# Moving eight transposition bursts on TensorE and one tanh on ScalarE in a two-layer hybrid SSD / gMLP step

## The chip, the cores and the metric

The kernel runs on one core of a Trainium2 chip. The metric is the device time of one execution in microseconds (us), the median of several runs. Engine names: TensorE (PE) does matmuls and transpositions and loads its weights beside them (PEld), VectorE (DVE) and ScalarE (ACT) work element by element, GpSimd (POOL) here only splits weights, SyncE (SP) and ScalarE issue transfers.

## The reference, cut to what matters

Two layers act on 640 tokens (128 context, 512 latent) of 1024 features. Each layer normalises, makes one wide input projection, and feeds two branches:

```python
h = rms_norm(x, norm_w) * (1 + scale[:, None]) + shift[:, None]
proj = h @ w_in
xbc_raw, z_m, dt_raw, u_raw, v_raw, z_g, gl_m, gl_g = split(proj)
# SSD branch: xs, bm, cm of 1024 + 512 + 512 channels
xbc = silu(dwconv(xbc_raw, conv_w, conv_b))          # 5 taps, centred
dt = softplus(dt_raw + dt_bias)
y = scan forward + scan backward + d_skip * xs       # chunks of 128 tokens
y_m = rms_norm(y * silu(z_m), ssm_norm_w)
# gMLP branch
v = layer_norm(gelu(v_raw), ln_w, ln_b)
y_g = gelu(u_raw) * (w_sp mixing of v over 128 tokens + b_sp) * silu(z_g)
merged = sigmoid(gl_m) * (y_m @ w_out_m) + sigmoid(gl_g) * (y_g @ w_out_g)
x = x + gate[:, None] * (merged @ w_out)
```

## The kernel before, in words

Every layer has 89 weight tiles p = 0 to 88, each 128 output channels of 1024 inputs. A float32 product is made of three products of rounded parts (`hi*hi`, `lo*hi`, `hi*lo`), so an ordinary tile (`tile`, L538, with `chunk`, L554) has 8 chunks of 3 x 2 = 6 matmuls of 320 columns: 48 matmuls. It accumulates in one of two PSUM buffers, `acc0` and `acc1`. Tile t takes them in turn by `acc_no(t)` (L53), and `acc_ready` (L501) makes TensorE wait on `acc_free` until the tile two turns back has been read out.

Tiles 0 to 24 are the first phase of a layer. Tile 1 is dt. `V_AT` (L43) lists the eight v tiles 4, 5, 10, 11, 16, 17, 23, 24: they are computed in pairs with tokens on the partitions (`v_tile`, L504), and a pair shares one `acc` buffer and half of a bank X1 or X3; ScalarE reads a pair out with one gelu of 1024 columns (L1117, which frees the buffer) and one of 256 (L1120, which raises `v_made`). The remaining sixteen, `CONV_AT` (L44), are conv tiles. For conv i ScalarE copies the tile to `raw` (L1139), VectorE makes five taps (L1549, L1551), ScalarE a tanh (`conv_tanh`, L1084 to L1089), and VectorE the product (L1567). In layer 1 the first three conv tiles are computed before the row scale is known and go another way to `raw` (`raw_conv`, L1034); `RAWT, NRAW = 4, 3` (L48) name them: tiles 0, 2 and 3. So in layer 1 the tanh of conv 2 belongs to tile 3.

The last eight convs, i = 8 to 15, give x0 to x7. VectorE writes each to one of two buffers, `xo[:, j % 2]`; a write for i >= 10 waits until x of two convs before has been transposed (`tp_ready`, L1565) and stored to memory (`xf_stored`, L1566). TensorE transposes x_j in five 128x128 pieces to banks X0 and X1 (`x_transposes`, L850; `transposes`, L715, L720), ScalarE copies them to `x_tok` (L964, L965) and issues two stores to `xf_dram` (L1081, L1082).

Where such side work stands within TensorE's tiles is a table: `X_AT` (L88) for the x transpositions, `A_AT` for the bursts that make the chunk states (`a_burst`, L749). An entry (p, k) means: inside tile p, after its chunk k; k = 8 is behind the tile's last chunk. The same table sets the order on ScalarE: at the end of its step for tile p it does `copies(p + 1)`, the copies of all bursts of tile p + 1. All engines run strictly in the order in which their code is written. GpSimd splits weights two tiles ahead, SyncE loads them.

ScalarE's functions live in tables, of which one set is loaded at a time: the program carries explicit ACT_TABLE_LOAD instructions where the next function is not in the set at hand.

Of the kernel before, what the change touches and what calls it, by code (L numbers as in the profile page):

```python
# [38 lines left out]
N_TILES = 1 + NCONV + 8 + 16 + 8 + 32 + 8  # L39
# [4 lines left out]
CONV_AT = tuple(p for p in range(25) if p != DT_AT and p not in V_AT)  # L44
# [3 lines left out]
RAWT, NRAW = 4, 3  # L48
# [10 lines left out]
def weight_at(p):  # L59
# [11 lines left out]
    if p >= T_ZM:  # L71
# [13 lines left out]
NU = len(A_UNITS)  # L85

A_AT = [(19 + a, 2) for a in range(7)] + [(26 + a // 3, 2 + 3 * (a % 3)) for a in range(14)]
X_AT = [(p + 2, 4) for p in CONV_AT[8:14]] + [(25, 3), (25, 6)]  # L88
V_BANK = (1, 1, 3, 1)
PBB_AT = (27, 8)  # L90
SP_AT = [(30, 4), (31, 4), (32, 4), (34, 4), (36, 4), (38, 4), (39, 6), (40, 6)]
# [1 line left out]
B_AT = [(T_G - 2, 4), (T_G - 1, 8)] + [(p, k + 1) for p, k in B_AT[2:]]  # L93
STANDS = sorted([(at, "a", n) for n, at in enumerate(A_AT)] + [(at, "x", n) for n, at in enumerate(X_AT)]
                + [(PBB_AT, "pbb", 0)]
# [63 lines left out]
def build(nc, xT, wts, wada, cT, bada, normw, finalw, ssmw, convw, dtb, alog, dskip, lnw, lnb,  # L159
# [126 lines left out]
    def sem(name):  # L286
        return ctx.enter_context(nc.semaphore(name))
# [23 lines left out]
    tp_ready, tp_out, ln_ready = sem("tp_ready"), sem("tp_out"), sem("ln_ready")  # L311
# [30 lines left out]
    def acc_of(t):  # L342
        return acc[acc_no(t) % 2]
# [16 lines left out]
    def evacuated(eng, t):  # L360

        eng.wait_ge(acc_free[acc_no(t) % 2], acc_no(t) // 2 + 1)
# [135 lines left out]
    def _(pe):  # L498
        mm = nc.tensor.matmul

        def acc_ready(t):  # L501
            pe.wait_ge(acc_free[acc_no(t) % 2], acc_no(t) // 2)

        def v_tile(t, half, ready=None, hooks=()):  # L504


            j = V_AT.index(t % N_TILES) // 2
            if half == 0:
                acc_ready(t)
                if j > 0:  # L510
                    pe.wait_ge(v_made, KC // 2 * (t // N_TILES) + j)
                if j == 3:
                    pe.wait_ge(tp_out, 8 * (t // N_TILES) + 6)
                if ready is not None:
                    pe.wait_ge(hpre_ready, 8 * (ready[2] + 1))
            a, s = acc_of(t), t % 2
            for i in range(KC // 2):
                k = KC // 2 * half + i
                if i % 2 == 0:
                    pe.wait_ge(w_split, WQ * t + 3 + i // 2)  # L520
                if ready is not None:
                    for r in ready[0:2]:
                        pe.wait_ge(r, 8 * ready[2] + k + 1)
                for c in range(NCH):
                    out = X[V_BANK[j]][:, 2 * P:4 * P] if c == NCH - 1 else \
                        a[:, c // 2, 2 * P * (c % 2):2 * P * (c % 2 + 1)]
                    for n, (w, x) in enumerate(((w_hi, h_hi), (w_lo, h_hi), (w_hi, h_lo))):
                        last = mm(out.rearrange("p (t n) -> p t n", t=2), x[:, k, P * c:P * (c + 1)],  # L528
                                  w[:, s, :].rearrange("p (t k n) -> p k t n", t=2, n=P)[:, i, :, :],
                                  start=(k == 0 and n == 0 and c % 2 == 0),  # L530
                                  stop=(k == KC - 1 and n == 2 and (c % 2 == 1 or c == NCH - 1)))
                    if i == KC // 2 - 1 and c == NCH - 1:
                        last.then_inc(tile_done, 1)
                    for at, hook in hooks:
                        if (at == 2 * i + 1 and c == 2) or (at == 2 * i + 2 and c == NCH - 1):
                            hook()
# [309 lines left out]
        for L in range(DEPTH):  # L846
# [3 lines left out]
            def x_transposes(j):  # L850
                pe.wait_ge(conv_done, NCONV * L + 9 + j)
                if X_AT[j][0] > V_AT[-1]:
                    pe.wait_ge(v_made, KC // 2 * (L + 1))
# [16 lines left out]
            for p in range(1 if L > 0 else DT_AT + 1, T_G):  # L870
# [7 lines left out]
                elif p in V_AT:  # L878
                    v_tile(T0 + p, V_AT.index(p) % 2, hooks=hooks,
                           ready=(hhi_ready, h_ready, L) if L > 0 and p < RAWT + 2 else None)  # L880
# [4 lines left out]
            for j in range(8):  # L885
                p = T_G + 2 * j
# [24 lines left out]
    def _(act):  # L911
# [3 lines left out]
        def free(t, ins):  # L915
            ins.then_inc(acc_free[acc_no(t) % 2], 1)
# [70 lines left out]
        for L in range(DEPTH):  # L987
# [13 lines left out]
            def dt_log():  # L1001
                act.wait_ge(dtu_ready, L + 1)
                A(dtx[:, 2, :, :], dtx[:, 1, :, :], ACT.Ln).then_inc(dtl_ready, 1)
# [80 lines left out]
            def conv_tanh(i):  # L1084
                n = NCONV * L + i
                act.wait_ge(cv_ready, n + 1)
                if n > 0:
                    act.wait_ge(conv_done, n)
                A(cvt[:, 0:CW], cv[:, i % 2, 0:CW], ACT.Tanh).then_inc(cvt_ready, 1)  # L1089
# [8 lines left out]
            for p in range(T_UZ):  # L1098
                t = T0 + p
                if L == 0 or p >= RAWT:  # L1100
                    act.wait_ge(tile_done, t + 1)
                if p == DT_AT:
                    if L == 0:
                        for dst, src in pieces(acc_of(t), *dt_row, L, 64):
                            last = A(dst, src, ACT.Identity, bias=dtb_sb[0:64, L:L + 1])
                        free(t, last)
                        evacuated(act, t)
                        act.sem_inc(dtrow_ready, 1)
                        conv_tanh(0)
                        dt_exp()  # L1110
                        dt_log()
                    continue
                if p in V_AT:
                    j, half = divmod(V_AT.index(p), 2)
                    if half == 1:
                        g = slice(2 * j, 2 * j + 2)
                        free(t, A(v_tok[:, g, 0:NCH - 1, :].rearrange("p g c n -> p c g n"),  # L1117
                                  acc_of(t)[:, :, :].rearrange("p b (c g n) -> p (b c) g n", c=2, n=P),
                                  ACT.Gelu_apprx_tanh))
                        A(v_tok[:, g, NCH - 1, :], X[V_BANK[j]][:, 2 * P:4 * P].rearrange("p (g n) -> p g n", n=P),  # L1120
                          ACT.Gelu_apprx_tanh).then_inc(v_made, 1)
                    if L > 0 and p == RAWT + 1:
                        conv_tanh(NRAW - 1)
                    copies(p + 1)
                    continue
                i = CONV_AT.index(p)
                if L > 0 and i < NRAW:
                    if i > 0:
                        raw_conv(i, p)
                        conv_tanh(i - 1)  # L1130
                        (dt_exp, dt_log)[i - 1]()
                        copies(p + 1)
                    continue
                if i >= 2:
                    act.wait_ge(cv_ready, NCONV * L + i - 1)
                else:
                    act.wait_ge(pads_ready, L + 1)
                for dst, src in pieces(acc_of(t), *raw_row(i), L):
                    last = A(dst, src, ACT.Copy)  # L1139
                free(t, last)  # L1140
                if i == (4, 5)[L]:
                    act.wait_ge(cum_ready, L + 1)
                    for d in range(2):
                        act.dma_start(cum_dram[L, NH * d:NH * (d + 1), :], cum_t[32 * d:32 * d + NH, :])\
                            .then_inc(cum_stored, 16)
                    act.wait_ge(ex_arg, L + 1)
                    A(ex[:, :, :, :], ex[:, :, :, :], ACT.Exp).then_inc(ex_ready, 1)
                    for rows in (slice(0, NH), slice(64, 64 + NH)):
                        A(c_buf[4][rows, :], cum_t[rows, :], ACT.Exp).then_inc(exr_ready, 1)
                    act.wait_ge(exr_ready, 2 * (L + 1))  # L1150
                    for d in range(2):
                        act.dma_start(ex_dram[L, :, d, :, :], c_buf[4][64 * d:64 * d + NH, :]).then_inc(ex_stored, 16)
                if i == 9:
                    act.dma_start(lnb_sb[:, :], lnb[L:L + 1, :].rearrange("l (k p) -> p (l k)", p=P),
                                  allow_slow_non_contiguous=True).then_inc(wsp_in, 16)
                    act.dma_start(states[0][:, :], h0[L, 0, :, :]).then_inc(st_in, 16)
                    act.dma_start(states[2 * (NCH - 2) + 1][:, :], h0[L, 1, :, :]).then_inc(st_in, 16)
                if L == 0 and i == 0:
                    continue
                copies(p + 1)  # L1160
                conv_tanh(i)
# [22 lines left out]
            for what, n in order_act():  # L1184
# [8 lines left out]
                elif what == "uz":  # L1193
                    t = T0 + T_UZ + n
# [13 lines left out]
                elif what == "glg":  # L1208
                    t = T0 + T_G + 2 * n
# [3 lines left out]
                else:  # L1213
# [6 lines left out]
                    if n < NU:  # L1220
# [4 lines left out]
                        for h in range(HPG):  # L1225
                            j = HPG * g + h
# [8 lines left out]
                        for h in range(HPG):  # L1235
                            j = NH + HPG * g + h
# [7 lines left out]
            for j in range(8):  # L1244
                t = T0 + T_ZM + j
# [13 lines left out]
            for j in range(8):  # L1259
                t = T0 + GLM_AT[j]  # L1260
# [676 lines left out]
```

## Time and profile before

| what | value |
|---|---|
| time, median of 3 (lowest to highest) | 1458.27 us (1458.12 to 1458.31) |
| time of the profiled execution | 1458.31 us |
| its span | 1456.2 us |
| TensorE busy | 1438.0 us, 99% |
| VectorE / ScalarE / GpSimd busy | 986.3 / 469.4 / 1029.5 us |
| TensorE clock over the run | 0.997 of full |

The profiled execution's own time is its span plus 2.1 us that lie around it. A row of the time line gives the start in us, the time in us that the row covers, the engine, the source line and operation, what it writes and reads, and the count; in brackets behind it stands how long the engine was idle before and who ended that.

### The profile page before, as it was taken

The page shows a single profiled execution, that of the slowest core. Times are in us where ns is not written, and L with a number is a line of the kernel's source. Part 1 is how long each engine was busy: PE and PEld are TensorE (multiplying, and loading weights), DVE is VectorE, ACT ScalarE, POOL GpSimd, SP SyncE. Part 2 cuts the span into 40 slices and gives each one's busy share as a digit, 9 for nine tenths or more (in the row PEclk, how much of TensorE's full clock was granted, in tenths as well). Part 3 has the DMA queues.
Part 4 walks back from the last instruction along what each step waited for, and adds up shares of the span by engine and source line. Part 5 has one row for each costly group of instructions (what it writes and reads, how often), then busy time and mean ns, then how long its engine had stood idle before and what let it go on. Part 6 is the DMA issues. An engine that isn't in the chain of part 4 may idle for free.

```text
span 1456.2 us, 26929 instructions
## 1 busy us (share of the span) xinstructions
PE 1438.0 (99%) x10127; PEld 1392.1 (96%) x10127; DVE 986.3 (68%) x1451; ACT 469.4 (32%) x1079; POOL 1029.5 (71%) x1431
## 2 busy tenths in 40 slices
PE   8999999999999999999999999999999999999996
PEld 5999998999999999999999999989999999999996
DVE  5865566674787678988869676567567885867234
ACT  4331222313666423001243323241256661310111
POOL 2688875596555489998868897658864556979762
PEclk9999999999999999999999999999999999999998
DMA  9112433113566465444342232411347655443222
GB/s 365 60 63 73 129 108 120 61 63 115 162 180 184 136 266 198 140 154 135 112 144 74 77 118 96 136 58 59 102 130 193 168 171 184 164 179 116 73 74 86
DMA packets 110988, 190.30 MB, mean 131 GB/s; under 512 B 10656, under 2 KB 72224, under 8 KB 109472
## 3 DMA queue, kind: packets, MB, share of 16 engines
q1 hardware_dynamic: 40448, 139.65, 28.8%
q10 hardware_dynamic: 70432, 49.11, 11.4%
q8 instruction: 80, 1.31, 0.4%
q14 instruction: 28, 0.23, 0.0%
HBM read 170.58 MB, written 18.15 MB: 130 GB/s over the span
## 4 chain that ended last, share of the span: by engine, by line
PE 95%; DVE 2%; issue 1%; POOL 0%; DMA 0%; ACT 0%; DVEq 0%; SPq 0%; POOLq 0%; ACTq 0%
PE acc L563 76%; PE acc L528 6%; PE X L795 2%; PE X L762 2%; PE X L787 2%; PE X L528 1%; PE X L827 1%; PE X L806 1%; PE X L720 1%; PE acc L573 1%; DVE cv L1551 1%; PE acc L679 0%; PE X L610 0%; DMA xr<-in_xT 0%; DVE xr L1852 0%
## 5 line engine op out<-in xcount | busy, mean ns | idle before, releaser
L466 POOL CAST w_hi<-w_st 128x256 fp32r<-128x256 f32 x708 | 413.7, 599 | 399.1 <-issue 180.7
L471 POOL TENSOR_TENSOR w_lo<-w_st,w_hi 128x256 fp32r<-128x256 f32 x708 | 653.3, 933 | 0.0
L563 PE MATMUL acc<-h_hi,w_hi 128*128 128x320 f32 x1744 | 406.3, 314 | 1.0 <-POOL w_lo L471 0.8
L563 PE MATMUL acc<-h_lo,w_hi 128*128 128x320 f32 x1744 | 397.8, 309 | 0.4 <-DVE h_lo L1408 0.4
L563 PE MATMUL acc<-h_hi,w_lo 128*128 128x320 f32 x1744 | 397.5, 309 | 0.0
L563 PEld LDWEIGHTS acc<-h_hi,w_hi 128*128 128x128 f32 x1744 | 288.6, 188 | 11.1 <-issue 7.6
L563 PEld LDWEIGHTS acc<-h_lo,w_hi 128*128 128x128 f32 x1744 | 291.5, 188 | 1.1 <-DVE h_lo L1408 0.9
L563 PEld LDWEIGHTS acc<-h_hi,w_lo 128*128 128x128 f32 x1744 | 291.4, 188 | 0.0
L1551 DVE SCALAR_TENSOR_TENSOR cv<-raw,convw_sb,cv 128x642 f32<-128x642 f32 x128 | 134.8, 1053 | 4.5
L1336 DVE SCALAR_TENSOR_TENSOR ada_acc<-ada_st,sc,ada_acc 128x512 f32<-128x512 f32 x112 | 103.4, 962 | 1.8
L1089 ACT ACTIVATE cvt<-cv 128x642 f32<-128x642 f32 x32 | 23.8, 743 | 159.4 <-DVE cv L1551 159.4
L528 PE MATMUL acc<-w_hi,h_hi 128*128 128x256 f32 x256 | 73.4, 287 | 0.3 <-POOL w_lo L471 0.3
L528 PE MATMUL acc<-w_hi,h_lo 128*128 128x256 f32 x256 | 72.4, 283 | 0.0
L528 PE MATMUL acc<-w_lo,h_hi 128*128 128x256 f32 x256 | 72.4, 283 | 0.0
L1632 DVE SCALAR_TENSOR_TENSOR gdt<-gm,tm,gdt 128x128 f32<-128x128 f32 x160 | 71.6, 507 | 1.1 <-ACT gdt L1237 0.8
L1532 DVE TENSOR_TENSOR xw<-x_tok,ex 128x256 f32<-128x256 f32 x80 | 46.0, 618 | 37.6 <-PE X L762 37.2
L1549 DVE TENSOR_SCALAR cv<-raw,convw_sb 128x642 f32<-128x642 f32 x32 | 27.3, 852 | 62.7 <-ACT raw L1139 62.6
L1227 ACT ACTIVATE dmat<-cum_bc,ncf 128x128 f32<-128x128 f32 x160 | 62.4, 390 | 15.3 <-issue 10.9
L1268 ACT ACTIVATE c_buf<-acc 128x640 f32<-128x640 f32 x16 | 11.3, 706 | 159.8 <-PE acc L563 159.8
L1229 ACT ACTIVATE cum_bc<-cum_bc,ebs 128x128 f32<-128x128 f32 x160 | 62.0, 387 | 0.0
L1237 ACT ACTIVATE gdt<-gm,tm 128x128 f32<-128x128 f32 x160 | 51.2, 391 | 27.8 <-DVE gm L1645 21.1
L563 PE MATMUL acc<-yg_hi,w_hi 128*128 128x320 f32 x256 | 60.1, 316 | 0.0
(256 smaller groups left out, 2493.9 us busy)
## 6 DMA issues: line engine op xcount, KB each, us to landing
w_st<-in_wts SPq DMA_DIRECT2D x178, 512.0 KB, 3.6
cum_bc<-cum_dram ACTq DMA_DIRECT2D x80, 256.0 KB, 5.0
ada_st<-in_wada SPq DMA_DIRECT2D x33, 512.0 KB, 4.3
ex_bc<-ex_dram ACTq DMA_DIRECT2D x64, 128.0 KB, 3.4
ada_pre<-in_wada SPq DMA_DIRECT2D x15, 512.0 KB, 13.2
mga_dram<-c_buf SPq DMA_DIRECT2D x16, 320.0 KB, 4.8
xf<-xf_dram SPq DMA_DIRECT2D x4, 1280.0 KB, 7.0
mga<-mga_dram SPq DMA_DIRECT2D x2, 2560.0 KB, 10.2
```

The costliest lines, as they stand in the source:

```text
L466: nc.gpsimd.tensor_copy(w_hi[:, slot, cols], w_st[:, slot, cols]).then_inc(s_pool, 1)
L471: nc.gpsimd.tensor_tensor(w_lo[:, slot, cols], w_st[:, slot, cols], f(w_hi[:, slot, cols]), ALU.subtract).then_inc(w_split, 1)
L528: last = mm(out.rearrange("p (t n) -> p t n", t=2), x[:, k, P * c:P * (c + 1)], w[:, s, :].rearrange("p (t k n) -> p k t n", t=2, n=P)[:, ...
L563: last = mm(a[:, hf, 0:n1], w[:, s, cols], x[:, k, hf * HALF:hf * HALF + n1], start=(k == 0 and n == 0), stop=(k == KC - 1 and n == 2))
L762: mm(X[3][:, cols], bt[:, s, :], xw[:, s, :, :, :].rearrange("p d h w -> p (d h w)")[:, cols], start=True, stop=True).then_inc(s_mm, 1)
L1227: last = A(dmat[:, n % 2, h, :], cum_bc[n % 2][:, 0, h, :], ACT.Identity, bias=ncf[:, c, j:j + 1])
L1229: last = A(cum_bc[n % 2][:, 1, h, :], cum_bc[n % 2][:, 1, h, :], ACT.Identity, bias=ebs[:, c, j:j + 1])
L1237: last = A(gdt[:, n % 2, h, :], gm[:, n % 2, 1, :], ACT.Copy, scale=tm[:, c, j:j + 1])
L1336: STT(out=o, in0=w, scalar=s, in1=o, op0=ALU.mult, op1=ALU.add)
L1532: last = TT(xw[:, a % 2, d, :, :], xg, per_head(ex[:, d, c, HPG * g:HPG * (g + 1)], HD), ALU.mult)
L1551: ins = STT(out=o, in0=r[:, tap:tap + CW], scalar=w[:, tap:tap + 1], in1=o, op0=ALU.mult, op1=ALU.add)
L1632: last = STT(out=gdt[:, s, h, :], in0=gm[:, s, 0, :], scalar=tm[:, c, j:j + 1], in1=gdt[:, s, h, :], op0=ALU.mult, op1=ALU.add)
```

## The change: what it does

Three edits.

1. `X_AT`: x0 to x4 move from behind chunk 4 to behind the last chunk of the same tile (15, 16, 17, 20, 21). x5 moves from tile 22, chunk 4, to tile 25, chunk 3; x6 from (25, 3) to (25, 5); x7 from (25, 6) to (25, 8).
2. `v_tile`: the wait on `tp_out` ahead of tile 23 goes. The `elif` changes nothing: `ready` is only given for the first pair.
3. ScalarE, layer 1: the tanh of conv 2 moves from behind the gelus of the pair 4, 5 to the step of tile 4, ahead of them.

```diff
-X_AT = [(p + 2, 4) for p in CONV_AT[8:14]] + [(25, 3), (25, 6)]
+X_AT = [(p + 2, 8) for p in CONV_AT[8:13]] + [(25, 3), (25, 5), (25, 8)]
...
                 if j > 0:
                     pe.wait_ge(v_made, KC // 2 * (t // N_TILES) + j)
-                if j == 3:
-                    pe.wait_ge(tp_out, 8 * (t // N_TILES) + 6)
-                if ready is not None:
+                elif ready is not None:
                     pe.wait_ge(hpre_ready, 8 * (ready[2] + 1))
...
                     j, half = divmod(V_AT.index(p), 2)
+                    if L > 0 and p == RAWT:
+                        conv_tanh(NRAW - 1)
                     if half == 1:
                         g = slice(2 * j, 2 * j + 2)
                         free(t, A(v_tok[:, g, 0:NCH - 1, :].rearrange("p g c n -> p c g n"),
...
                           ACT.Gelu_apprx_tanh).then_inc(v_made, 1)
-                    if L > 0 and p == RAWT + 1:
-                        conv_tanh(NRAW - 1)
                     copies(p + 1)
```

First place: ScalarE in layer 1, from the copy of tile 3 on, before the change. `cvt<-cv` is a conv's tanh, `dtx` the logarithm for dt, `v_tok` a gelu, `raw` the copy of a conv tile.

```order
L1037 ACTIVATE raw_71<-c_buf2_89,bsh_143 128x5x64
L1089 ACTIVATE cvt_73<-cv_72 128x642 [waits conv_done,cv_ready]
L1003 ACT_TABLE_LOAD
L1003 ACTIVATE dtx_94<-dtx_94 128x160 [waits dtu_ready]
L1117 ACT_TABLE_LOAD [waits tile_done]
L1117 ACTIVATE v_tok_55<-acc1 128x4x2x128 [waits tile_done]
L1120 ACTIVATE v_tok_55<-X1 128x2x128
L1089 ACTIVATE cvt_73<-cv_72 128x642 [waits conv_done,cv_ready]
L1139 ACTIVATE raw_71<-acc0 128x128 [waits cv_ready,tile_done]
```

The same stretch of ScalarE with the change (lines move by two).

```order
L1035 ACTIVATE raw_71<-c_buf2_89,bsh_143 128x5x64
L1087 ACTIVATE cvt_73<-cv_72 128x642 [waits conv_done,cv_ready]
L1001 ACT_TABLE_LOAD
L1001 ACTIVATE dtx_94<-dtx_94 128x160 [waits dtu_ready]
L1087 ACT_TABLE_LOAD [waits conv_done,cv_ready]
L1087 ACTIVATE cvt_73<-cv_72 128x642 [waits tile_done]
L1117 ACT_TABLE_LOAD
L1117 ACTIVATE v_tok_55<-acc1 128x4x2x128 [waits tile_done]
L1120 ACTIVATE v_tok_55<-X1 128x2x128
L1137 ACTIVATE raw_71<-acc0 128x128 [waits cv_ready,tile_done]
```

The tanh of conv 2 now stands ahead of the gelu that reads `acc1`, a third table load has come in, and the load ahead of the tanh carries the waits of the tanh.

Second place: TensorE, the border of tiles 6 and 7 in layer 1; these rows are the same before and with the change (here before).

```order
L563 MATMUL acc0<-h_hi_49,w_lo_54 128x320 x2
L563 MATMUL acc0<-h_lo_50,w_hi_53 128x320 x2
L563 MATMUL acc1<-h_hi_49,w_hi_53 128x320 [waits w_split,acc_free1]
L563 MATMUL acc1<-h_hi_49,w_hi_53 128x320
L563 MATMUL acc1<-h_hi_49,w_lo_54 128x320 x2
```

Tile 7 writes `acc1`, which the pair 4, 5 has used, and its first matmul waits for the release of that buffer.

Third place: TensorE in tile 25 (buffer `acc1` in layer 0) with the change, from the burst behind its third chunk on. L718 is a transposition burst.

```order
L718 MATMUL X1<-ident_118,xo_74 128x128 [waits tp_out,v_made,conv_done]
L718 MATMUL X0<-ident_118,xo_74 128x128 x4
L561 MATMUL acc1<-h_hi_49,w_hi_53 128x320 x2
L561 MATMUL acc1<-h_hi_49,w_lo_54 128x320 x2
L561 MATMUL acc1<-h_lo_50,w_hi_53 128x320 x2
L561 MATMUL acc1<-h_hi_49,w_hi_53 128x320 [waits w_split]
L561 MATMUL acc1<-h_hi_49,w_hi_53 128x320
L561 MATMUL acc1<-h_hi_49,w_lo_54 128x320 x2
L561 MATMUL acc1<-h_lo_50,w_hi_53 128x320 x2
L718 MATMUL X1<-ident_118,xo_74 128x128 [waits tp_out,v_made,conv_done]
L718 MATMUL X0<-ident_118,xo_74 128x128 x4
```

Before, the first of these bursts was x6, and x7 followed three chunks behind it; now they are x5 and x6, two chunks apart, and x7 closes the tile.

## Rows read from the trace of the kernel before

**Rows 1.** The page: busy time (us, share of span), and the chain's shares.

```profile
PE 1438.0 (99%) x10127; PEld 1392.1 (96%) x10127; DVE 986.3 (68%) x1451; ACT 469.4 (32%) x1079; POOL 1029.5 (71%) x1431
PE 95%; DVE 2%; issue 1%; POOL 0%; DMA 0%; ACT 0%; DVEq 0%; SPq 0%; POOLq 0%; ACTq 0%
```

**Rows 2.** Waits of TensorE, whole span: waiter, releaser, us, times, longest.

```profile
PE acc L617 <- DVE sel L1382: 3.2, 1, 3.2
...
PE X L762 <- ACT bt L1074: 0.5, 2, 0.2
```

**Rows 3.** Time line of TensorE, layer 1, around the starts of tiles 6 and 7.

```profile
783.26 0.28 PE L528 MATMUL X<-w_hi,h_lo 128*128 128x256 f32 x1
783.38 0.46 PE L563 MATMUL acc<-h_hi,w_hi 128*128 128x320 f32 x2
...
790.42 0.46 PE L563 MATMUL acc<-h_hi,w_hi 128*128 128x320 f32 x2
```

**Rows 4.** Time line of ScalarE, 783 to 799 us.

```profile
784.16 1.28 ACT L1003 ACT_TABLE_LOAD   x1
785.46 0.34 ACT L1003 ACTIVATE dtx<-dtx 128x160 f32<-128x160 f32 x1
785.81 1.28 ACT L1117 ACT_TABLE_LOAD   x1
787.11 1.03 ACT L1117 ACTIVATE v_tok<-acc 128x1024 f32<-128x1024 f32 x1
...
794.19 0.74 ACT L1089 ACTIVATE cvt<-cv 128x642 f32<-128x642 f32 x1 [5.78 <-DVE cv L1551]
794.83 1.32 ACT L1139 ACTIVATE raw<-acc 128x128 f32<-128x128 f32 x3
```

**Rows 5.** Time line of VectorE, 783 to 796 us.

```profile
785.83 1.15 DVE L1487 RECIPROCAL dtx<-dtx 128x160 f32<-128x160 f32 x1 [0.39 <-ACT dtx L1003]
...
789.46 0.61 DVE L1549 TENSOR_SCALAR cv<-raw,convw_sb 128x642 f32<-128x642 f32 x1
790.10 4.05 DVE L1551 SCALAR_TENSOR_TENSOR cv<-raw,convw_sb,cv 128x642 f32<-128x642 f32 x4
```

**Rows 6.** Busy us by engine; the PEclk column after POOL is the granted clock.

```profile
0.00:5.00 5.00, 1.77 (x4) 1.51 (x5) 1.08 (x6) 1.50 (x2) 2.00 (x13) 1.00 0.55 163
...
1446.00:1447.00 1.00, 0.54 (x3) 0.30 (x3) 0.80 (x3) 0.17 (x1) 0.00 (x0) 1.00 0.00 0
1447.00:1448.00 1.00, 0.00 (x0) 0.00 (x0) 1.00 (x3) 0.00 (x0) 0.00 (x0) 0.53 0.00 0
```

**Rows 7.** Time line of TensorE, layer 0, tile 25: burst x6; start of tile 26.

```profile
226.54 0.71 PE L720 MATMUL X<-ident,xo 128*128 128x128 f32 x5
...
232.03 0.46 PE L563 MATMUL acc<-h_hi,w_hi 128*128 128x320 f32 x2
```

**Rows 8.** Time line of ScalarE, layer 0, 223 to 231 us.

```profile
225.32 0.40 ACT L1120 ACTIVATE v_tok<-X 128x256 f32<-128x256 f32 x1
...
227.47 0.59 ACT L964 ACTIVATE x_tok<-X 128x512 f32<-128x512 f32 x1
227.75 0.49 ACTq L1082 DMA_DIRECT2D xf_dram<-xo  x1
227.95 0.28 ACT L965 ACTIVATE x_tok<-X 128x128 f32<-128x128 f32 x1
```

**Rows 9.** Time line of VectorE, layer 0: four of its waits.

```profile
175.21 1.07 DVE L1549 TENSOR_SCALAR cv<-raw,convw_sb 128x642 f32<-128x642 f32 x1 [12.92 <-ACT raw L1139]
...
217.21 1.10 DVE L1532 TENSOR_TENSOR xw<-x_tok,ex 128x256 f32<-128x256 f32 x2 [6.42 <-PE X L762]
...
224.12 1.17 DVE L1567 SCALAR_TENSOR_TENSOR xo<-cvt,cv 128x642 f32<-128x642 f32 x1 [0.81 <-ACT cvt L1089]
...
234.50 0.61 DVE L1532 TENSOR_TENSOR xw<-x_tok,ex 128x256 f32<-128x256 f32 x1 [7.44 <-PE X L762]
```

**Rows 10.** L1082, the store issued at 227.75 us: issue to landing.

```profile
DMA to landing us min/median/max: 2.2/2.2/2.2
```

**Rows 11.** L1082, the store issued at 230.8 us: issue to landing.

```profile
DMA to landing us min/median/max: 4.7/4.7/4.7
```

## The prediction

> **What bounds the kernel now.** I read the page's busy times and its chain first: TensorE is busy 99% of the span and carries 95% of the chain that ends last [rows 1]. So a microsecond counts only if TensorE loses or gains it. TensorE's waits come next: in the whole span the longest is 3.2 us at the start, and in mid-kernel there is hardly one; the two at the burst L762, for `bt`, make 0.5 us together [rows 2]. There is almost nothing to win by removing waits, and all to lose by adding one. Third, the time line of each engine where the three edits act: layer 1 at tiles 4 to 7, and tiles 15 to 25 in both layers.
>
> **The tanh that moves (edit 3).** What TensorE does is fixed. The pair 4, 5 ends and tile 6 starts at 783.38; tile 7 starts at 790.42, 48 matmuls and 7.04 us later, without a wait, 147 ns for each matmul [rows 3]. Tile 7 writes `acc1`, the buffer of the pair 4, 5, so it may start only when the gelu of 1024 columns has read that buffer. Before, ScalarE does that gelu at 787.11 for 1.03 us, so it ends at 788.14, 2.3 us ahead of tile 7 [rows 4].
>
> With the change the gelu stands behind the tanh of conv 2. That tanh needs the last tap of conv 2 on VectorE, whose taps start at 790.10 and last 4.05 us, to 794.15 [rows 5]. Can VectorE be earlier? Conv 2 starts at 789.46, behind the dt arithmetic that waits at 785.83 for the logarithm of ScalarE [rows 5]. The logarithm stands ahead of both orders and does not move, so 794.15 stays. The order on ScalarE with the change is then: a table load that itself carries the wait for conv 2, the tanh, a second table load, the gelu. With the durations of [rows 4]:
>
> - load from 794.19 (this is when the tanh starts today), 1.28 us and a gap of 0.02: 795.49
> - tanh 0.74, gap 0.02: 796.25
> - load 1.28, gap 0.02: 797.55
> - gelu 1.03: 798.58; then TensorE about 0.05 later: 798.63.
>
> Tile 7 would have started at 790.42. The stall is 8.2 us, all on the path, as TensorE has no wait ahead that could take it back. Behind it nothing is late in turn. ScalarE's 256-column gelu and the copy of tile 6 (1.32 us, [rows 4]) are done near 800.3, VectorE starts conv 3 some 4 us later than today and TensorE runs 8 us later than today, so all who feed TensorE have gained on it. GpSimd has split the weights already.
>
> One rule speaks against these durations. The Trainium skill, "ScalarE: Activation LUTs", section "What ACT_TABLE_LOAD costs", adds to a load of 1283 ns a drain of about 1380 ns, 2.66 us for each switch. The trace agrees with the first part and not with the second: a load starts at 784.16 and the next function at 785.46, a second load at 785.81 and the gelu at 787.11 [rows 4]. By its figure the stall would be 11.0 us; the sum goes by the rows.
>
> **The clock behind the stall.** TensorE then stands idle for 8.2 us. The trace shows that its clock falls when it has little to do: granted 1.00 in the slice from 1446, with the engine 54% busy, and 0.53 in the next one, in which it has nothing [rows 6]. That is the step from 2.4 to 1.2 GHz. No row shows busy work at the lower level. The bounds: nothing, if the clock is not lowered or comes back at once (in the first 5 us of the kernel it is granted 1.00, though the engine waits for 3.2 us of them [rows 2, 6]); at most the rest of a whole tile at the lower level, where 320 columns take 267 ns in place of 133, so 48 x 0.133 = 6.4 us. I take 15 of the 48 matmuls, 2.0 us, nearer to the lower end because the kernel's first row shows a full clock so near an idle stretch. The Trainium skill, "TensorE: Matmul & The Clock Gate", section "Loop structure matters more than you think", says that such a wait leaves the array at the lower clock and that the matmuls behind it run cold; it gives no other sum than the one above.
>
> **The bursts that move (edit 1).** The bursts are the same work, eight of five transpositions for each layer. A burst holds TensorE for about half a microsecond wherever it stands; I see nothing in its place that makes it cheaper but a shared border at tiles 15 and 17, which I put at 0.1 us for both layers together. What can cost are its waits.
>
> - x0 to x4: their copies come half a tile (3.5 us) later on ScalarE and hold back the tanh of the conv behind. For x0 to x2 the 12.92 us in which VectorE is idle until 175.21 swallow that, for x3 and x4 the 6.42 us until 217.21 [rows 9]. 0 us.
> - x5 takes the place of x6 at (25, 3): same wait on `v_made`, raised at 225.72 [rows 8], 0.8 us ahead of 226.54 [rows 7]. 0 us.
> - x6 two chunks later, 0.54 + 6 x 0.293 = 2.3 us behind x5, so at 228.85 on this clock. The copies of x5 end at 228.23 [rows 8]: 0.6 us to spare. 0 us.
> - x7 behind the last chunk, at 232.03, where tile 26 starts today [rows 7]. It needs conv 15 finished. Today VectorE writes it at 224.12 [rows 9]; now the same buffer still holds x5, so VectorE waits until x5 is transposed and stored. The store of x5 is issued where that of x6 is today, 227.75 [rows 8], and that one lands 2.2 us later [rows 10]: 229.95, plus the write of 1.17 [rows 9] and 0.05: 231.2. 0.8 us to spare. 0 us.
> - Queued behind that write on VectorE are the two state weightings of L1532. The second waits for TensorE until 234.50 anyway, with 7.44 us idle [rows 9]; the first is done by 232.5. 0 us. On ScalarE the loads of `wsp` and `pbb` are issued some 2 us later; they are needed in tile 27, two tiles on.
>
> **The wait that goes (edit 2).** TensorE never waits there today [rows 2], and the bursts around it are done before. 0 us.
>
> **The sum.** 8.2 + 2.0 - 0.1 = 10.1 us on the profiled execution's 1458.31 (span 1456.2 and 2.1 around it): 1468.4. The median of the runs, 1458.27, is 0.04 off that, so I forecast 1468.3.
>
> **Rivals.**
>
> - *The clock costs nothing.* For it: the full clock in the first row. Against it: the fall at 1447 [rows 6]. 1458.3 + 8.2 - 0.1 = 1466.4.
> - *x7 waits for the store of x5.* The next store of this kind took 4.7 us [rows 11], just ahead of two loads of 512 KB on the same queue. If x5's does, the write ends at 227.75 + 4.7 + 1.17 + 0.05 = 233.7 against 232.03, 1.6 us in each layer, 3.3 in all, on top of the stall: 1471.6. Against it: at x5's time those loads are not yet issued.
> - *A drain behind each table load.* If the loads around the tanh behave unlike those of [rows 4], 2 x 1.38 more: 1471.1.
> - *Not slower: tile 7 does not depend on that gelu.* Place: the first matmul of tile 7. If the release that it counts came from another read-out, already made at 790.42, the moved tanh would be hidden: tile 8 only starts past 798 and the gelu would be done near 798.6. Then only the 0.1 us remains: 1458.2. It decides at whether the tile two turns back is the pair 4, 5; the order shows `acc1` in both, which speaks against it.
> - *It does not do what it says.* The tanh of conv 2 is meant to come sooner, but it starts with the last tap in either order, so in no case does it.
>
> **Chances.** Forecast (the stall, and a clock that costs between 0.5 and 6.4 us) 0.77; clock free 0.09; store 0.05; drain 0.04: together 0.95 for slower. A measurement of this kernel tells 0.2%, 2.9 us, from no change. The not-slower case has 0.05, of which I give 0.04 to same and 0.01 to faster, for a gain that I don't see. The range reaches from just below the free clock, 1465.8, to 1471.8, past the store and drain cases; it leaves out the upper end of the clock's bound (1472.7) and the not-slower case.
>
> **What would show it.** In the profile after: one idle stretch of TensorE of about 8.2 us ahead of tile 7 in layer 1, released by ScalarE's gelu L1117; a granted clock near 0.5 in the slices right behind it and matmuls 280 ns apart there; on ScalarE near 794 load, tanh, load, gelu; no wait at the bursts of tile 25; the same spacing as before in layer 0, up to half a microsecond. The prediction is wrong if tile 7 starts on time, if the idle stretch is much over 8.5 us, or if waits appear at the bursts of tile 25.

## The result, and the profile after

The changed kernel takes 1471.86 us, the median of 4 runs (1471.79 to 1472.11), against 1458.29 us (4 runs, 1458.12 to 1458.45) for the kernel before beside it. The ratio is 1.0093 with a 95% interval of 1.0076 to 1.0111: slower by some 13.6 us. Forecast were 1468.3 us and a range of 1465.8 to 1471.8, so the sign was right, the size was 3.5 us too small, and the median lies 0.06 us past the upper end of the range. The profiled execution took 1472.30 us with a span of 1470.2, that is 13.99 us more than the 1458.31 of before.

The page of the changed kernel has the same work on every engine, as in [rows 1]: TensorE is 3.8 us busier with the same 10127 instructions, and ScalarE has one instruction more, the second table load. In the chain ACT and DMA, 0% each before, have 1% each.

```profile
PE 1441.8 (98%) x10127; PEld 1395.1 (95%) x10127; DVE 988.0 (67%) x1451; ACT 470.2 (32%) x1080; POOL 1022.5 (70%) x1431
...
PE 92%; DVE 4%; DMA 1%; issue 1%; ACT 1%; POOL 0%; ACTq 0%; DVEq 0%; SPq 0%; POOLq 0%
```

The waits of TensorE in the whole span (waiter, releaser, us, times, longest), beside [rows 2], have two lines that were not there: the first, and the third. The others are those of before, to some tenths of a microsecond; one of 0.8 us in the opening is put down to `w_lo` before and to `h_hi` after.

```profile
PE acc L561 <- ACT v_tok L1117: 8.0, 1, 8.0
PE acc L615 <- DVE sel L1380: 3.2, 1, 3.2
PE X L718 <- DVE xo L1565: 2.6, 2, 1.3
...
PE X L760 <- ACT bt L1072: 0.4, 2, 0.2
```

**The first: tile 7 of layer 1.** The time line of ScalarE in the changed kernel, which answers to [rows 4]:

```profile
785.64 1.28 ACT L1001 ACT_TABLE_LOAD   x1
786.94 0.34 ACT L1001 ACTIVATE dtx<-dtx 128x160 f32<-128x160 f32 x1
795.67 1.28 ACT L1087 ACT_TABLE_LOAD   x1 [8.39 <-DVE cv L1549]
796.96 0.74 ACT L1087 ACTIVATE cvt<-cv 128x642 f32<-128x642 f32 x1
797.72 1.28 ACT L1117 ACT_TABLE_LOAD   x1
799.01 1.02 ACT L1117 ACTIVATE v_tok<-acc 128x1024 f32<-128x1024 f32 x1
```

The table load itself waits for VectorE's last tap, whose line is `791.57 4.03`, against `790.10 4.05` in [rows 5]. Between 787.28 and 795.67 ScalarE does nothing, with the gelu that TensorE needs queued behind. The time line of TensorE in the changed kernel, which answers to [rows 3]:

```profile
791.61 0.46 PE L561 MATMUL acc<-h_lo,w_hi 128*128 128x320 f32 x2
800.09 0.90 PE L561 MATMUL acc<-h_hi,w_hi 128*128 128x320 f32 x2 [8.03 <-ACT v_tok L1117]
800.79 0.74 PE L561 MATMUL acc<-h_hi,w_lo 128*128 128x320 f32 x2
...
805.05 0.74 PE L561 MATMUL acc<-h_hi,w_hi 128*128 128x320 f32 x2
805.59 0.68 PE L561 MATMUL acc<-h_hi,w_lo 128*128 128x320 f32 x2
806.10 0.45 PE L561 MATMUL acc<-h_lo,w_hi 128*128 128x320 f32 x2
806.39 0.46 PE L561 MATMUL acc<-h_hi,w_hi 128*128 128x320 f32 x2
```

Everything here stands 1.48 us later than before, from layer 0, so tile 7 was due at 790.42 + 1.48 = 791.90. It starts at 800.09: 8.19 us. Behind it, after a first pair of 0.70 us, a pair of matmuls takes 0.53 us until 806, then 0.29 us. The windows of the changed kernel (the column of the granted clock follows POOL's, as in [rows 6]) say why:

```profile
794.00:795.00 1.00, 0.00 (x0) 0.00 (x0) 0.96 (x2) 0.00 (x0) 1.00 (x2) 1.00 0.00 0
795.00:796.00 1.00, 0.00 (x0) 0.00 (x0) 0.60 (x1) 0.33 (x1) 1.00 (x2) 0.91 0.00 0
796.00:797.00 1.00, 0.00 (x0) 0.00 (x0) 0.00 (x0) 0.99 (x2) 1.00 (x3) 0.50 0.00 0
...
805.00:806.00 1.00, 1.00 (x5) 1.00 (x5) 0.84 (x1) 0.12 (x1) 0.00 (x0) 0.50 0.00 0
806.00:807.00 1.00, 1.00 (x9) 1.00 (x8) 0.35 (x1) 0.62 (x1) 0.00 (x0) 0.97 0.00 0
```

The clock is at its lower level (1.2 GHz) from 795.8, that is 3.8 us after TensorE's last work, to 806.1, 6.0 us after its first. Some 22 matmuls run slowly. The last matmul of tile 7 starts 2.78 us later than the spacing of before would put it.

**The second: burst x7 of tile 25, in both layers.** The chain of waits of the changed kernel in 226 to 233.7 us (start, us, what):

```profile
227.00 0.16 ACTq L1079
227.16 0.03 ACT x_tok L962
227.19 4.51 DMA xf_dram<-xo
231.70 0.03 issue
231.73 0.05 DVEq L1564
231.78 0.05 issue
231.83 1.03 DVE xo L1565
232.86 0.04 issue
232.91 0.77 PE X L718 x5
```

TensorE's row for the burst ends with `[1.29 <-DVE xo L1565]`. The store of x5 takes 4.51 us, not the 2.2 of [rows 10], and VectorE writes conv 15 over x5 only after that. The burst comes 1.46 us late in layer 0, and 1.47 in layer 1, where that landing takes 4.7.

What was different for the store: its neighbour. SyncE's row in 218 to 236 us, changed kernel:

```profile
219.29 7.83 SPq L380 DMA_DIRECT2D w_st<-in_wts  x2
```

and before:

```profile
219.88 8.83 SPq L380 DMA_DIRECT2D w_st<-in_wts  x2
```

Each row holds two issues; the second, a load of 512 KB of weights for tile 27, is at 226.79 in the changed kernel and was at 228.38. The two parts of the store of x5 are issued at 226.79 and 227.19: in the very same moment. SyncE is released by GpSimd, which splits the weights of tile 26. Its casts at that place, changed kernel:

```profile
223.97 0.39 POOL L466 CAST w_hi<-w_st 128x256 fp32r<-128x256 f32 x1
...
224.99 0.39 POOL L466 CAST w_hi<-w_st 128x256 fp32r<-128x256 f32 x1
```

and before:

```profile
224.56 0.99 POOL L466 CAST w_hi<-w_st 128x256 fp32r<-128x256 f32 x1
...
226.19 0.59 POOL L466 CAST w_hi<-w_st 128x256 fp32r<-128x256 f32 x1
```

Before, VectorE was writing conv 15 at 224.12 [rows 9], and then weighting states. After, it stands idle for 9.1 us, waiting for the store; the casts take 0.39 us each, which makes GpSimd 1.0 us faster over the tile. Another 0.59 us come from the schedule, as the burst of x5 no longer stands in tile 22. So the load was 1.6 us early.

**The sum in the trace.** 8.19 (stall) + 2.78 (clock) + 1.46 + 1.47 (x7) = 13.90; the start of the last 384-column matmul moves from 1443.15 to 1457.15, by 14.00. The 0.1 left is small shifts of both signs.

### The profile page after: what moved, and what is told of

Same layout as the page of the kernel before. It is cut to its first block, busy times and chain, and to the rows that moved or that the text cites. A ratio compares the mean times of both kernels' runs of the same rounds, so it can differ in the third digit from the quotient of the medians.

```text
span 1470.2 us, 26927 instructions
## 1 busy us (share of the span) xinstructions
PE 1441.8 (98%) x10127; PEld 1395.1 (95%) x10127; DVE 988.0 (67%) x1451; ACT 470.2 (32%) x1080; POOL 1022.5 (70%) x1431
## 4 chain that ended last, share of the span: by engine, by line
PE 92%; DVE 4%; DMA 1%; issue 1%; ACT 1%; POOL 0%; ACTq 0%; DVEq 0%; SPq 0%; POOLq 0%
PE acc L561 74%; PE acc L526 5%; PE X L793 2%; PE X L760 2%; PE X L785 2%; DVE cv L1549 1%; PE X L526 1%; PE X L825 1%; PE X L804 1%; DMA xf_dram<-xo 1%; PE acc L571 1%; PE acc L677 0%; PE X L718 0%; PE X L608 0%; DVE xr L1850 0%
## 5 line engine op out<-in xcount | busy, mean ns | idle before, releaser
L466 POOL CAST w_hi<-w_st 128x256 fp32r<-128x256 f32 x708 | 409.2, 592 | 420.1 <-PE acc L561 191.9
## 6 DMA issues: line engine op xcount, KB each, us to landing
ada_pre<-in_wada SPq DMA_DIRECT2D x15, 512.0 KB, 13.6
```

Of the source, the lines that this page charges most:

```text
L466: nc.gpsimd.tensor_copy(w_hi[:, slot, cols], w_st[:, slot, cols]).then_inc(s_pool, 1)
```

## The experiments

Ratios are against the kernel before, timed beside each variant. Their 95% intervals reach 2.5 us to either side in the runs of four, and most of them overlap the changed kernel's. Effects of 2 to 3 us are therefore read from one trace of each kernel, with the medians beside it.

**The tanh alone** (the kernel before, with edit 3 only).

```diff
+                    if L > 0 and p == RAWT:
+                        conv_tanh(NRAW - 1)
                     if half == 1:
...
-                    if L > 0 and p == RAWT + 1:
-                        conv_tanh(NRAW - 1)
```

> Edit 3 alone: the tanh of conv 2 ahead of the gelu in layer 1; bursts and waits as before. Theory (three costs that add): an idle stretch of TensorE of 8.2 us ahead of tile 7 in layer 1, released by ScalarE's gelu, and behind it 2.8 us lost at the lower clock, so 1458.3 + 11.0 = 1469.3 us, and no wait at the bursts of tile 25. Rival (the costs hang together, so that the waits at tile 25 come from the shifted schedule that the stall leaves): 1469.3 plus at least one wait at tile 25 in layer 1, 1470.8. A second rival (the stall hides a part that would be lost elsewhere): under 1467.

Measured: 1468.69 us, ratio 1.0068 (1.0051 to 1.0085). Span 1466.2, 10.0 over before. TensorE's waits in it:

```profile
PE acc L563 <- ACT v_tok L1119: 8.0, 1, 8.0
```

The idle stretch is 8.20 us, and the clock takes 2.02. This is the stall and its clock by themselves; x7 does not wait. Here the lower level ends 4.3 us after the first matmul, and 6.0 us in the changed kernel.

**The bursts alone** (the kernel before, with edits 1 and 2 only).

```diff
-X_AT = [(p + 2, 4) for p in CONV_AT[8:14]] + [(25, 3), (25, 6)]
+X_AT = [(p + 2, 8) for p in CONV_AT[8:13]] + [(25, 3), (25, 5), (25, 8)]
...
-                if j == 3:
-                    pe.wait_ge(tp_out, 8 * (t // N_TILES) + 6)
-                if ready is not None:
+                elif ready is not None:
```

> Edits 1 and 2 alone: the x bursts in their new places, the wait of tile 23 gone, the tanh where it was before. Theory: TensorE waits at burst x7 in both layers, about 1.46 us each, for VectorE's write of conv 15, which waits for the landing of the store of x5: 1458.3 + 2.9 = 1461.2 us. What I said before the run (0.8 us to spare at x7): 1458.2. Rival that the long store came from layer 1's shift only: one wait, 1459.8.

Measured: 1461.60 us (10 runs), ratio 1.002 (1.001 to 1.003). TensorE's waits at the bursts:

```profile
PE X L718 <- DVE xo L1565: 2.6, 2, 1.3
```

The landing of the store of x5 in layer 0, issued at 226.9 us:

```profile
DMA to landing us min/median/max: 4.6/4.6/4.6
```

The wait at x7 belongs to the bursts and needs nothing of the tanh. It costs 1.46 + 1.47 us, and the landing is slow here too. The two halves, 10.0 and 2.7 us of span, make 12.7 of the 14.0. Of the rest 0.8 is the clock's 2.78 against 2.02. The last 0.5 lies in the opening of the kernel, which none of the edits touches: at 30 us TensorE was already 0.18 and 0.36 us ahead of before in these two traces, and 0.04 in the changed kernel's.

**TensorE kept busy in the stall, 15 matmuls** (the changed kernel; useless work into a free bank).

```diff
+        def fill(n):
+            for _ in range(n):
+                mm(X[3][:, 0:2 * P], ident[:, :], tri[:, :, :].rearrange("p d n -> p (d n)"), start=True, stop=True)
...
+                if L > 0 and p == 6:
+                    fill(15)
```

> The changed kernel with 15 matmuls of no use (fp32, 256 columns, into a bank that nobody reads then) between tiles 6 and 7 of layer 1, where TensorE would stand idle. By the rows of the opening each takes about 0.49 us, 7.3 us together, so they end before the gelu does. Theory (2.8 us of the loss is the clock, which falls in the idle stretch): granted clock stays at 1.00, the matmuls of tile 7 are 147 ns apart at once, 1471.9 - 2.8 = 1469.1 us. Rival (matmuls behind a stall are slow for another reason than idleness, such as the buffers): 1471.9, no change.

Measured: 1469.82 us, ratio 1.0073 (1.0056 to 1.0089), 2.0 us under the changed kernel. Time line of TensorE in it (each of the 15 float32 matmuls is two instructions, so the row counts 30):

```profile
792.01 6.64 PE L620 MATMUL X<-tri,ident 128*128 128x256 f32 x30
800.20 0.56 PE L561 MATMUL acc<-h_hi,w_hi 128*128 128x320 f32 x2 [1.56 <-ACT v_tok L1124]
800.60 0.45 PE L561 MATMUL acc<-h_hi,w_lo 128*128 128x320 f32 x2
```

Tile 7 starts 8.20 us late as before, since the gelu is no earlier, but from the second pair on a pair takes 0.29 us and the granted clock is 1.00 throughout. Of the 2.78 us only 0.10 stay, in the first pair (0.40 us), so 0.1 belongs to starting again after a wait and the rest to the clock. That the slow stretch comes from the idling and from nothing else that the change did is shown, in the traces of both kernels. The median gained 2.0 us where 2.8 were expected: in this execution 0.4 us were lost again behind the last 384-column matmul, at the end of the kernel.

**10 of these matmuls** (the same, `fill(10)`).

> The changed kernel with 10 matmuls of no use between tiles 6 and 7 of layer 1, 4.9 us, so that TensorE stands idle for about 3.3 us ahead of tile 7. In the changed kernel the granted clock fell only some 3.9 us after the last matmul, and came back 5.9 us after the first. Theory (a shorter idle stretch does not lower the clock): clock 1.00 throughout, as with 15 matmuls, 1469.1 to 1469.8 us. Rival (any stretch of some us does): 2 to 3 us more.

Measured: 1472.06 us, ratio 1.0095 (1.008 to 1.0111). The profiled execution (1470.0 us) has an idle stretch of 3.7 us and a clock of 1.00 throughout:

```profile
PE acc L561 <- ACT v_tok L1124: 3.7, 1, 3.7
```

Its other three runs took 1471.65 to 1472.93 us, from 0.2 us under the median of the changed kernel to 1.1 us over it. No trace of them is kept. So the theory holds for the one execution with a trace, while the times of the other three are those of the rival. Both can be true: in the five traces with a fall, the clock stayed at 1.00 for 2.1 to 5.2 us after TensorE's last work (2.1 with the tanh alone, 5.2 with x7 in its own buffer), and 3.7 lies between. Whether the clock fell in the other three runs stays open.

**x7 in its own buffer** (the changed kernel; the readers of x7 take `xo7` as well).

```diff
+    xo7 = place("xo7", [P, PITCH], r_uz + 7 * TOK * 4)
...
-                    dst = xo[:, i % 2, 0:CW]
-                    if i >= 10:
+                    dst = xo[:, i % 2, 0:CW] if i < 15 else xo7[:, 0:CW]
...
+                    if 10 <= i < 15:
```

> The changed kernel with a buffer of its own for x7, in memory that is free at that time, so that VectorE's write of conv 15 need not wait until x5 is transposed and stored. Theory (the two waits at x7 come from the shared buffer): VectorE writes conv 15 at once when its tanh is done, no wait at tile 25, 1471.9 - 2.9 = 1469.0 us. Rival (the last burst waits for the copies of x6 or for something at the tile's border): 1471.9.

Measured: 1468.42 us, ratio 1.0064 (1.0047 to 1.008), 3.4 us under the changed kernel. Time line of VectorE in it, to be read beside [rows 9]: conv 15 is written right behind its tanh again.

```profile
223.59 1.17 DVE L1571 SCALAR_TENSOR_TENSOR xo<-cvt,cv 128x642 f32<-128x642 f32 x1 [0.81 <-ACT cvt L1090]
```

The wait at x7 is gone in both layers: what it waited for was the buffer. The span, 1466.3, is 3.9 us under the changed kernel's, 2.93 for the waits and 0.90 for a clock that costs 1.88 here.

This run also settles what made the load early. It has the bursts and stores of the changed kernel, but VectorE is at work again while GpSimd splits the weights of tile 26. The two casts at that place:

```profile
224.02 0.99 POOL L467 CAST w_hi<-w_st 128x256 fp32r<-128x256 f32 x1
...
225.65 0.59 POOL L467 CAST w_hi<-w_st 128x256 fp32r<-128x256 f32 x1
```

They are as long as in the kernel before. The load for tile 27:

```profile
227.84 0.33 SPq L381 DMA_DIRECT2D w_st<-in_wts  x1
```

It comes 1.04 us later than in the changed kernel, 0.64 us behind the store of x5, and that store lands after 2.2 us, as in [rows 10].

**The weight load held back until x5 is stored** (the changed kernel, on SyncE ahead of the load for tile 27).

```diff
+            if p == T_UZ + 2:
+                sp.wait_ge(xf_stored[1], 32 * (KC // 2 * L + 3))
             weight(t, t % 2)
```

> The changed kernel; SyncE issues the load of weight tile 27 only when both stores of x5 have landed, in both layers. Theory (in the changed kernel the store of x5 takes 4.5 us because the load of weight tile 27 is issued in the same tenth of a microsecond; before, that load came 0.6 us behind the store at the same place): the larger store lands about 2.2 us after its issue, VectorE writes conv 15 some 2.3 us earlier, no wait at x7, 1471.9 - 2.9 = 1469.0 us. Rival (the store is slow for another reason, the stores of the chunk states ahead of it on the same queue): landing stays 4.5 us, 1471.9 us.

Measured: 1469.06 us, ratio 1.0076 (1.0059 to 1.0092); span 1466.2, 4.0 under the changed kernel's, with a clock cost of 1.83. The landing of the store of x5, issued at 227.2 us:

```profile
DMA to landing us min/median/max: 2.2/2.2/2.2
```

And VectorE's write of conv 15, from its time line:

```profile
229.53 0.83 DVE L1567 SCALAR_TENSOR_TENSOR xo<-cvt,cv 128x642 f32<-128x642 f32 x1 [6.72 <-DMA xf_dram<-xo]
```

With the buffer shared and nothing but the load moved, the landing is 2.2 us again, conv 15 is written at 229.53 and x7 comes on time. The prediction's own figures (229.95 and the write behind it) hold when the load is out of the way. That the load at the same moment makes the store slow is shown. The load now falls together with the store of x6 (229.45 against 229.48), and there it is that store which takes 4.7 us.

**Both table loads out of the way** (the changed kernel; a gelu of one column ahead of the moved tanh, so that the table that holds both is loaded while ScalarE waits anyway).

```diff
                     if L > 0 and p == RAWT:
+                        own.link(A(warm[:, :], eps_sb[:, :], ACT.Gelu_apprx_tanh))
                         conv_tanh(NRAW - 1)
```

> The changed kernel with a gelu of one column ahead of the moved tanh, so that the table set that holds both gelu and tanh is loaded while ScalarE waits for conv 2 anyway; the two loads between conv 2 and the gelu go. Theory (the stall is conv 2's end plus load, tanh, load, gelu): tanh at 794.2 in the clock of before, gelu ends 2 x 1.30 us earlier, stall 8.2 - 2.6 = 5.6 us; the clock still falls, and costs 2 to 2.8 us: 1471.9 - 2.6 = 1469.3 us. Rival (the stall is set by when VectorE or ScalarE turn to something else): 1471.9.

Measured: 1469.44 us, ratio 1.0077 (1.006 to 1.0094). Time line of ScalarE in it:

```profile
787.46 1.28 ACT L1114 ACT_TABLE_LOAD   x1
788.75 0.20 ACT L1114 ACTIVATE warm<-eps_sb 128x1 f32<-128x1 f32 x1
795.85 0.74 ACT L1087 ACTIVATE cvt<-cv 128x642 f32<-128x642 f32 x1 [6.90 <-issue]
796.50 1.01 ACT L1118 ACTIVATE v_tok<-acc 128x1024 f32<-128x1024 f32 x1
```

No load stands between the last tap and the gelu. The stall falls from 8.19 to 5.49 us, so the two loads made 2.70 of it, 1.35 each with what lies around them. By the Trainium skill ("ScalarE: Activation LUTs", "What ACT_TABLE_LOAD costs"), with its drain, taking two loads away would have saved 5.3 us, an estimate from its 2.66 us for each switch; this run does not agree. The clock still costs 2.16.

**Bursts x0 to x5 at the ends of their tiles, everything else as before.**

```diff
-X_AT = [(p + 2, 4) for p in CONV_AT[8:14]] + [(25, 3), (25, 6)]
+X_AT = [(p + 2, 8) for p in CONV_AT[8:14]] + [(25, 3), (25, 6)]
```

> The kernel before with x0 to x5 behind the last chunk of their tiles (x5 in tile 22), x6 and x7 and the tanh where they were, the wait of tile 23 kept. What I reckoned for shared borders: 0.1 us less than before. Theory: no wait of TensorE anywhere new, 1458.2 to 1458.4 us. Rival (the copies that come half a tile later hold up conv 12 to 15 and with them the copy of bt at tile 25): 1458.8 or more, with a longer wait at L762.

Measured: 1461.06 us (11 runs), ratio 1.0017 (1.0008 to 1.0026). Not expected at all. Time line of TensorE:

```profile
206.13 0.71 PE L720 MATMUL X<-ident,xo 128*128 128x128 f32 x5
207.90 0.35 PE L528 MATMUL acc<-w_hi,h_hi 128*128 128x256 f32 x1 [1.06 <-ACT x_tok L965]
```

With x5 behind tile 22, tile 23 waits for ScalarE's copy of it: the wait that edit 2 removes, 1.3 us a layer. So edit 2 costs nothing because edit 1 moves x5 past it, and the change swaps this wait for the one of 1.46 us a layer at x7. The ends of tiles save nothing: 0.02 us.

**The copies for tile 24 ahead of the tanh of conv 15** (the kernel before; my attempt at the 0.5 us of [rows 2]).

```diff
-                    copies(p + 1)
+                    if p != V_AT[6]:
+                        copies(p + 1)
...
                 copies(p + 1)
+                if i == NCONV - 1:
+                    copies(p + 2)
                 conv_tanh(i)
```

> The kernel before with ScalarE's copies for tile 24 (the chunk state and bt) moved ahead of the tanh of conv 15, for which ScalarE waits 13.1 us. Before, TensorE waits at the burst of tile 25 for that bt, 0.4 us over the spacing in each layer. Theory: both waits go and nothing comes for them, 1458.3 - 0.8 = 1457.5 us. Rival (the wait only changes its releaser, to the state weighting of VectorE): 1458.3.

Measured: 1457.74 us (11 runs) against 1458.56 (21 runs), ratio 0.9996 (0.9987 to 1.0005). In the trace TensorE gains 0.48 us in layer 0 and 0.49 in layer 1 at tile 25, and the wait for `bt` is gone. The interval holds 1: the best kernel of the study by its median, but by less than the runs can tell apart.

## Why the prediction was right in sign and short in size

- **The stall**: right, 8.19 us against 8.2. Load, tanh, load, gelu stand as forecast, each within 0.1 us of its row. The 1.28 us loads of [rows 4] carry over, without a drain behind them, also where the load itself waits.
- **The clock**: the mechanism was right, the size was off: a term of 2.0 us (15 matmuls), and 2.78 us (22) in this execution. Without x7's waits it was 2.02, 1.88 and 1.83, with them but a shorter stall 2.16. In all five it is 0.1 us for the start and 45% of the time worked at the lower level, since a pair takes 0.53 us in place of 0.29. That time was 6.0 us here and 4.3, 4.0, 3.9 and 4.6 in the others; what sets it no run here shows. It is 0.8 us of the miss.
- **Burst x7**: here the prediction failed, at "0.8 us to spare. 0 us". The step behind it, that the store "lands 2.2 us later [rows 10]", took a landing time from another moment of the trace. The chain that it named was right (store of x5, VectorE's write, x7), the landing was 4.5 us, and it cost 2.9 us in both layers. The rival for it priced 3.3, but I gave it 0.05, as the two loads on ScalarE's queue were not yet issued. The load that mattered was on SyncE's queue, and in the trace of before it was issued 1.6 us later (SyncE's rows above); I had looked at the store's own queue only. What was missing is a consequence of the prediction's own wait: VectorE idle ahead of conv 15 makes GpSimd's casts shorter, and they release that load.
- **Bursts x0 to x6**: right. x5 and x6 do not wait, x0 to x2 move the time by 0.02 us. The 0.1 us for shared borders is not there.
- **The wait of tile 23**: 0 us is right for the change. "TensorE never waits there today" was no proof of it; alone with x5 at the end of tile 22 that wait costs 1.3 us a layer.
- **Behind the stall**: right, nothing else is late. x7's lateness in layer 1 comes in full on top.

The term for the clock came near the other four (1.83 to 2.16 us) by luck, for its reason does not hold. The prediction leaned to the lower end "because the kernel's first row shows a full clock so near an idle stretch", and it held that "no row shows busy work at the lower level". The opening is such work. TensorE in the kernel before, the matmuls of line L617 alone, all of one shape (the column of the granted clock follows PEld's):

```profile
4.00:6.00 2.00, 2.00 (x6) 1.55 (x6) 1.00 1.01 415
8.00:10.00 2.00, 2.00 (x11) 1.76 (x10) 1.00 0.97 376
```

Up to 6.3 us they stand 0.43 us apart and then 0.22, the ratio of the two levels, although the column says 1.00 in both windows. So the full clock of the first row is no evidence of one, neither for this term nor for the rival that the clock costs nothing.

The profiled execution missed the sum of 10.1 us by 3.9: 2.9 at x7, 0.8 in the clock, and 0.1 for the borders that give nothing. The medians stand 0.4 us closer.

## To carry to other kernels

A reader that moves behind a slow producer in an in-order queue carries all that is queued behind it: take the producer's end, add every step of the queue to it, and compare with the time at which the buffer is wanted. When a margin rests on the landing of a transfer, look at what all queues issue within its own time, and at who could release those issues sooner; a duration read where the neighbours were quiet is a lower bound. And a stall of several microseconds on TensorE costs more than itself, here 1.8 to 2.8 us, as long as nothing keeps the clock up.

## What the runs showed of the hardware that I had not expected

- A store of 256 KB landed after 2.2 us, and after 4.5 to 4.9 us when 512 KB of weights were issued on another queue at the same moment or 0.4 us ahead of it; held back by 2.7 us, or only 0.64 us behind the store, the load left it at 2.2.
- A cast of 256 columns on GpSimd took 0.39 us with VectorE idle and 0.59 and 0.99 us at the same place with VectorE at work. An idle VectorE thus moved a DMA by a microsecond; in the run with x7 in its own buffer VectorE was at work there, and the load was back behind the store. The Trainium skill, "SBUF — State Buffer", section "SBUF: two separate sides", states that VectorE and GpSimd share a pair of ports, held by one instruction at a time where VectorE reads two inputs from SBUF; these rows agree: the long casts start while VectorE's product for conv 15 and its state weighting run.
- Behind stalls of 5.5 to 8.2 us the granted clock was still 0.50 for the first 3.9 to 6.0 us of work, and it had fallen 2.1 to 5.2 us after the last work. In one and the same kind of stall both differed from kernel to kernel.
- In the first 6 us of the kernel the profile's column of the granted clock says 1.00 while equal matmuls stand 0.43 us apart, and 0.22 us later on.
- The table load ahead of the moved tanh waited for the data of that tanh (8.39 us idle, then 1.28 us of load). One useless gelu ahead of the wait moved it out of the way and removed the second load as well, since the table that it loads serves both functions.
